# Row norms from products with ones and block products of 64 columns, in a two-layer diffusion backbone

## The reference

```python
def rmsnorm(x, g):
    y = x * rsqrt(mean(x * x, axis=-1) + 1e-6)
    return y * g
a = rmsnorm(x, norm_g) * (1 + scale) + shift
```

```python
q_dec, k_inv = q * exp(b), k * exp(-b)        # b: running sum of log gates in the chunk
att = where(tril, q_dec @ k_inv.T, 0)         # 64 x 64 in each chunk
o = att @ v + q_dec @ state_before_chunk
```

## Time and profile before

| | us |
|---|---|
| median of 3 runs | 1732.68 (1732.04 to 1733.84) |
| profiled execution, own time | 1733.48 |
| its span in the trace | 1731.8 |
| PE busy | 1633.6 (94%) |
| DVE busy | 621.9 (36%) |
| POOL busy | 601.2 (35%) |
| ACT busy | 516.8 (30%) |
| mean granted clock of PE | 0.968 |

### The profile page before, as it was taken

The page is one execution under the profiler, slowest core; times in us unless marked ns, Lnnn a source line. Parts: engine busy times, 40 slices in busy tenths (PEclk is TensorE's granted clock), DMA queues, the critical chain, the costliest instruction groups (busy, mean ns, idle before and its releaser), DMA issues. The chain is left out here.

```text
span 1731.8 us, 22476 instructions
## 1 busy us (share of the span) xinstructions
PE 1633.6 (94%) x9900; PEld 1371.8 (79%) x9900; DVE 621.9 (36%) x731; ACT 516.8 (30%) x560; POOL 601.2 (35%) x434
## 2 busy tenths in 40 slices
PE   6999999998799999999999997999977899999997
PEld 3888787877588888888888886788865688888885
DVE  5543334443441121211211125769985411111112
ACT  4343243322231110111111122477772321121122
POOL 2122211212213232332423244144464355455452
PEclk9899999999899999999999998999998899999999
DMA  9223334222224333233323222022212133333322
GB/s 338 82 86 110 88 84 122 74 74 80 67 73 123 98 98 98 89 107 101 105 87 98 92 89 88 25 73 73 72 50 73 49 98 97 98 97 98 97 79 79
DMA packets 199316, 160.63 MB, mean 93 GB/s; under 512 B 7234, under 2 KB 193972, under 8 KB 199220
## 3 DMA queue, kind: packets, MB, share of 16 engines
q1 hardware_dynamic: 198832, 159.08, 29.8%
q10 hardware_dynamic: 388, 0.12, 0.0%
HBM read 157.08 MB, written 2.10 MB: 92 GB/s over the span
## 5 line engine op out<-in xcount | busy, mean ns | idle before, releaser
L492 POOL TENSOR_TENSOR w_lo<-raw,w_hi 128x512 fp32r<-128x512 f32 (+1 forms) x404 | 580.8, 1469 | 1103.9 <-ACT w_hi L963 1103.9
L541 PE MATMUL duo<-a_hi,w_hi 128*128 128x512 f32 x1648 | 493.6, 360 | 36.9 <-DVE a_lo L1535 17.9
L544 PE MATMUL duo<-a_lo,w_hi 128*128 128x512 f32 x1648 | 486.8, 355 | 0.0
L547 PE MATMUL duo<-a_hi,w_lo 128*128 128x512 f32 x1648 | 486.1, 355 | 0.0
L963 ACT ACTIVATE w_hi<-raw 128x2048 fp32r<-128x2048 f32 (+1 forms) x101 | 192.5, 1906 | 577.1 <-PE duo L547 576.7
L541 PEld LDWEIGHTS duo<-a_hi,w_hi 128*128 128x128 f32 x1648 | 271.1, 191 | 96.9 <-issue 45.7
L544 PEld LDWEIGHTS duo<-a_lo,w_hi 128*128 128x128 f32 x1648 | 271.2, 191 | 45.6
L547 PEld LDWEIGHTS duo<-a_hi,w_lo 128*128 128x128 f32 x1648 | 270.5, 191 | 45.7
L1587 DVE TENSOR_TENSOR hid<-duo,gate 128x1024 f32<-128x1024 f32 (+1 forms) x33 | 33.5, 1044 | 525.5 <-PE duo L547 525.5
L541 PE MATMUL duo<-h_hi,w_hi 128*128 128x512 f32 (+1 forms) x528 | 159.4, 356 | 0.0
L547 PE MATMUL duo<-h_hi,w_lo 128*128 128x512 f32 (+1 forms) x528 | 158.3, 354 | 0.0
(11 more groups left out here) (230 smaller groups left out, 1494.4 us busy)
## 6 DMA issues: line engine op xcount, KB each, us to landing
raw<-in_ffn_w_dram SPq DMA_DIRECT2D x120, 512.0 KB, 4.8
mod_ring<-in_w_mod_dram SPq DMA_DIRECT2D x80, 512.0 KB, 5.3
raw<-in_gla_w_in_dram SPq DMA_DIRECT2D x24, 512.0 KB, 4.8
raw<-in_lru_w_in_dram SPq DMA_DIRECT2D x16, 512.0 KB, 4.3
raw<-in_ffn_w_dram SPq DMA_DIRECT2D x16, 384.0 KB, 3.7
mod_first<-in_w_mod_dram SPq DMA_DIRECT2D x4, 1024.0 KB, 14.2
mod_second<-in_w_mod_dram SPq DMA_DIRECT2D x4, 1024.0 KB, 13.7
raw<-in_gla_w_out_dram SPq DMA_DIRECT2D x8, 512.0 KB, 5.1
```

The costliest lines, as they stand in the source:

```text
L492: pool.tensor_tensor(w_lo[b][:, k:k + 2, 0:cols], raw[b][:, k:k + 2, 0:cols], w_hi[b][:, k:k + 2, 0:cols].bitcast(F32), ALU.subtract).then ...
L541: pe.matmul(tile_out(ps, t, part, n), wh, act_hi[:, k, s:s + n], start=opens, stop=False, skip_group_check=True)
L544: pe.matmul(tile_out(ps, t, part, n), wh, act_lo[:, k, s:s + n], start=False, stop=False, skip_group_check=True)
L547: mm = pe.matmul(tile_out(ps, t, part, n), wl, act_hi[:, k, s:s + n], start=False, stop=last, skip_group_check=True)
```

## The change

For the norms:

- The fourth pair of tiles is no longer added on DVE. Its tiles are squared one by one, the first already when its own residual addition is done (new semaphore tile_added). PE multiplies a full block of ones (128 by 128) with sqsum and with the two squares, accumulating in PSUM, which gives the sum on all partitions at once (norm_sums). The small products, the reciprocal, the diagonal and the spreading product are gone.
- ACT turns the sum into the inverse root in place in PSUM, as exp(-0.5 ln(sum/1024 + eps)), for each part of the columns in turn; the table loaded ahead is the one with both functions.
- In ACT's residual_loop the last squares now come before the rounding of the coming weight chunk (and before a row copy), where they came after.
- sqsum is not cleared; the first pair is added directly. In the first norm PE now does all sums before the second section's products.

For the attention:

- att is computed as 64 by 64 blocks, one per chunk and direction (24 a head), at two column positions; its tile has half the columns, and so have the memset, the masked copies and the addition on DVE.
- The product of att with v_tok becomes two blocks per pair of chunks, each of 64 rows and 64 columns, on the diagonal of the array.
- POOL copies the mask's other half instead of clearing two corners.

```diff
-            def token_sums(n, parts):
+            def norm_sums(n, parts):
                 q = ("stat", n)
-                pe.wait_ge(summed, SUMMED[n])
                 duo_wait(q)
-                for t in range((parts[-1][1] + parts[-1][2]) // P):
-                    mm = pe.matmul(duo(q)[:, 1, 2 * t:2 * t + 2], sqsum[:, t * P:(t + 1) * P], ones[:, 0:2], start=True,
-                                   stop=True, skip_group_check=True)
-                mm.then_inc(token_summed, 1)
-
-            def spread(n, parts):
-                q = ("stat", n)
-                pe.wait_ge(diag_ready, n + 1)
-                for part, s, w in parts:
-                    mm = pe.matmul(tile_out(duo(q), 0, part, w), ones[:],
-                                   rdiag[:, s // P:(s + w) // P].rearrange("p t n -> p (t n)"), start=True, stop=True)
+                for i, src in enumerate((sqsum, sq[1][:, 0], sq[1][:, 1])):
+                    if i:
+                        pe.wait_ge(squared, 5 * n + 3 + i)
+                    else:
+                        pe.wait_ge(summed, 3 * n + 3)
+                    for part, s, w in parts:
+                        mm = pe.matmul(tile_out(duo(q), 0, part, w), ones[:], src[:, s:s + w], start=i == 0, stop=i == 2,
+                                       skip_group_check=True)
                 done(mm)
...
-            token_sums(0, BOTH)
+            norm_sums(0, BOTH)
             pe.wait_ge(mod_ready, 1)
             second_products(0)
-            spread(0, BOTH)
...
                 for j in range(12):
                     d, tau = j // 6, j % 6
-                    mm = pe.matmul(flat(q)[:, j * P:(j + 1) * P], k_inv[:, d, tau * P:(tau + 1) * P],
-                                   q_dec[:, d, tau * P:(tau + 1) * P], start=True, stop=True, skip_group_check=True)
+                    for c in range(2):
+                        n = 2 * tau + c
+                        mm = pe.matmul(flat(q)[CHUNK * c:CHUNK * (c + 1), j * CHUNK:(j + 1) * CHUNK],
+                                       k_inv[:, d, n * CHUNK:(n + 1) * CHUNK], q_dec[:, d, n * CHUNK:(n + 1) * CHUNK],
+                                       start=True, stop=True, tile_position=(0, CHUNK * c), skip_group_check=True)
...
                 for tau in range(TT):
-                    pe.matmul(flat(q)[:, tau * 256:(tau + 1) * 256], att[:, tau], v_tok[:, tau], start=tau % 2 == 0,
-                              stop=False, skip_group_check=True)
+                    for c in range(2):
+                        r = CHUNK * c
+                        pe.matmul(flat(q)[r:r + CHUNK, tau * 256:(tau + 1) * 256], att[r:r + CHUNK, tau],
+                                  v_tok[r:r + CHUNK, tau], start=tau % 2 == 0, stop=False, tile_position=(r, r),
+                                  skip_group_check=True)
...
-            def square(pair, n, width):
-                if pair >= 2:
-                    act.wait_ge(summed, pair - 1)
-                act.activation(sq[pair % 2][:, :, 0:width], xres[:, 2 * n:2 * n + 2, 0:width], ACT.Square
-                               ).then_inc(squared, 1)
+            def square(norm, n, width):
+
+                if n >= 2:
+                    act.wait_ge(summed, 3 * norm + n - 1)
+                if n < 3:
+                    act.activation(sq[n % 2][:, :, 0:width], xres[:, 2 * n:2 * n + 2, 0:width], ACT.Square
+                                   ).then_inc(squared, 1)
+                    return
+                for t in range(2):
+                    if t == 0 and norm:
+                        act.wait_ge(tile_added, norm)
+                    elif norm:
+                        wait_moved(act, (("out", 0, 3), ("w2", 0, 2, 3), ("out", 1, 3))[norm - 1])
+                    act.activation(sq[1][:, t, 0:width], xres[:, 6 + t, 0:width], ACT.Square).then_inc(squared, 1)
 
             def prep(layer, which, parts):
 
                 n = 2 * layer + which
-                q = ("stat", n)
-                act.wait_ge(token_summed, n + 1)
-                tiles = (parts[-1][1] + parts[-1][2]) // P
-                act.activation(rms[:, 0, 0:tiles], duo(q)[:, 1, 0:2 * tiles:2],
-                               ACT.Sqrt, bias=eps[:, 0:1], scale=1.0 / D).then_inc(rooted, 1)
+                wait_done(act, ("stat", n))
+                for part, s, w in parts:
+                    ps = tile_psum(("stat", n), 0, part)
+                    steps.link(act.activation(ps, ps, ACT.Ln, bias=eps[:, 0:1], scale=1.0 / D))
+                    act.activation(ps, ps, ACT.Exp, scale=-0.5).then_inc(rooted, 1)
...
                 for n, name in enumerate(names):
                     ahead = {v: k for k, v in CH.items()}.get(CH[name] + 2)
+                    if norm is not None and n == 3:
+                        square(norm, n, width)
                     if ahead is not None:
                         high(ahead, name)
                     if of == ("out", 0) and n == 3:
                         row_copy(6, 0)
-                    wait_moved(act, name)
-                    if pair is not None:
-                        square(pair + n, n, width)
+                    if norm is None or n < 3:
+                        wait_moved(act, name)
+                    if norm is not None and n < 3:
+                        square(norm, n, width)
...
-            act.preload_act_table_set("sqrt_and_others")
+            act.preload_act_table_set("natural_log_exp_and_others")
             prep(0, 1, BOTH)
...
-                tiles = width // P
-                dve.wait_ge(rooted, n + 1)
-                steps.link(dve.reciprocal(rms[:, 1, 0:tiles], rms[:, 0, 0:tiles]))
-                if n == 0:
-                    dve.wait_ge(consts_made, 1)
-                dve.tensor_tensor(rdiag[:, 0:tiles], ident[:].unsqueeze(1).broadcast_to([P, tiles, P]),
-                                  rms[:, 1, 0:tiles].unsqueeze(2).broadcast_to([P, tiles, P]), ALU.mult
-                                  ).then_inc(diag_ready, 1)
                 wait_done(dve, ("stat", n))
+                dve.wait_ge(rooted, ROOTED[n] + len(parts))
...
-            def residual_loop(of, layer, place_, parts, pair=None, permuted=False):
-                if pair is not None:
-                    clear_sum()
+            def residual_loop(of, layer, place_, parts, norm=None, permuted=False):
```

70 lines of the change are left out of this document (35 added, 35 removed).

## The result

The changed kernel takes **1712.8 us** (median of four runs, 1710.97 to 1715.97) against 1732.36 of the kernel before beside it (1730.04 to 1733.84). The ratio is 0.989, its 95% interval 0.9871 to 0.9909: 19.6 us less, with the interval reaching from about 16 to 22. A second series of the same kernel on another chip gave 1712.14 and 0.9869. The profiled execution took 1713.71, against 1733.48 before: 19.8 less, and that is the difference that the traces have to explain.

The account below looks back on a forecast made before the run. PE was taken as the bound, busy 1633.6 of 1731.8 us. Terms -5.4 - 5.9 - 3.7 + 1.0 - 0.7 - 0.4 = -15.1, with 0.8 off the profiled 1733.48, gave 1717.6 us; range 1711 to 1727.

Parts of the forecast that it names:

- Second norm, 5.4: Second norm: first normed tile at 466.75 instead of 472.15, 5.4 us less, with ACT last and PE 2 us earlier.
- Third, 5.9: Third norm: first normed tile at 1074.55 instead of 1080.48, 5.9 us less, by the same chain without a row copy.
- Fourth, 4.1 less 0.4: Fourth norm: normed tile 4.1 us earlier, less 0.4 for a_lo running beside POOL's w_lo work, so 3.7 less.
- First norm, +1.0: First norm: sums ahead of the second section's products start the main products 1.0 us later, bounds 0 and +4.1.
- Clearing the sum, 0.7: Ahead of the first residual additions: the memset of 0.70 us goes, 0.7 less.
- Heads, 0.4: Attention heads: att 0.15 less, v_tok blocks 0.15 less, block form changes 0.2 more; four heads 0.4 us less.
- A: Heads: block loads go side by side, att 1.3 instead of 2.6 us per head, 5.2 less over four, 1712.4; chance 0.17.
- The clock, no gain counted: Behind the norms: main products again begin at the lower level, 1.2 of 2.4 GHz, so no gain there.
- Rival B: Norms: the clock falls while squares are awaited and PE ends last; norms gain less, first norm +3, 1722.5; chance 0.16.
- C: Heads: the blocks' weight loads aren't hidden; four heads cost +24.4 us instead of -0.4, 1742.4; chance 0.06.
- D: Norms: logarithm and exponential don't share a table; ten more loads of 1.28, 13 us, 1730; chance 0.02.

Follow-up runs that it names:

- e9: The changed kernel once more, with nothing changed, for a second time and trace: 1712.14 us, ratio 0.9869 of the kernel before.
- e3: The changed kernel with all 24 att blocks of a head at one column position (half of att wrong): 1719.83 us, one run.
- e2: The kernel before with only the two block products of the heads from the change, norms untouched: 1728.21 us, ratio 0.9978.
- e4: The changed kernel with ACT rounding the next weights before the last squares and copying the row behind the exponentials: 1709.21 us, ratio 0.9859.
- e5: The changed kernel with 14 unused products of 256 columns behind the sums of norms two to four: 1712.05 us, ratio 0.9884.
- e10: The kernel of e11 with unused products in three further gaps of PE (6, 4 and 30): 1701.9 us, ratio 0.9818 of before.
- e11: The changed kernel with rounding before squares, section products before first sums, nine unused products per later norm, earlier DVE start on latent columns; second series: 1706.0 us, 0.9841.

## Why the prediction was right

The forecast of 1717.6 had the side and, within the range of 1711 to 1727, the time; it was 4.8 us too slow, and the 1712.8 lie below the 1714 to 1722 that I gave the forecast as summed. By its own steps, in the one pair of traces:

- **Second norm, 5.4:** 5.8 measured. The second square ended 3.07 us after the start of the last additions (455.75), as forecast (460.6 - 457.53). Rounding, row copy and table load ended at 6.67, not 6.82. The four PSUM passes took 2.16 with the last hop, not 2.4: that is the mis-sized part, 0.24. PE wasn't last, by 1.7 us (forecast 2).
- **Third, 5.9:** 6.3. **Fourth, 4.1 less 0.4:** 4.3 at the normed tile, less 0.55 for the a_lo beside POOL's work (1.30 instead of 0.75), and 3.7 at PE: as forecast, by the mechanism forecast.
- **First norm, +1.0:** +1.6, inside the bounds of 0 and 4.1. The sums ended at 32.78 instead of 32.3 and the section's products at 34.64 instead of 34.0. In the trace of after it is gone at 97 us, at least 1.1 of it by the clock within the v products; in e9, the same kernel, it isn't. I had carried a delay at the start through to the end without asking what lies between, and that varies by 2.4 us between executions with the same start.
- **Clearing the sum, 0.7:** 0.9.
- **Heads, 0.4:** 3.4. This is the step that missed, and the one rival that came true (A). The price of 0.055 per record for att is right for blocks at one position (0.059 in e3), and wrong for alternating ones (0.030). The group gave 1.15 us a head in three heads and 0.26 in the first, where a wait for k_tok of 0.72 took its place. The v_tok blocks gave 0.05 each, not 0.15. I had both ends of the term (1.3 and 2.6; 1.55 came) and chose the wrong one. Even with it, 48 x 0.055 = 2.64 against 24 x 0.112 = 2.69 is 0.05 less and not 0.15. The row that I set aside as unable to tell, the narrow blocks of the earlier trace rows at 0.026, was the nearest after all; it too has more than one column position, though no run tested that for blocks of 32 columns. And the claim that no row shows two loads side by side was true of the rows and not of the trace, in which L792's loads start in pairs.
- **The clock, no gain counted:** the forecast was that the main products begin at the lower level, and they do. In the pair of traces 3.2 us instead of 6.1 of them ran low, worth 1.6; but the same gap left 5.4 in e3 and the old gap 4.3 in e2, so this is not shown to be a gain of the change.
- **Not foreseen:** 2.5 us lost in the first FFN. It took away most of what the missed part of the heads gave. So some of the nearness of 1717.6 and 1712.8 is luck: without it the kernel would have been at about 1710, below my range (1712.8 - 2.5, an estimate from the traces). The clock ahead of head 0 and behind the second norm was luck the other way, up to 3.3 us; without either the kernel would have been near 1713.6 (an estimate again).

Terms and measurement: -15.0 in three norms became -15.7; -0.1 ahead of them became -4.9; then -1.6 by the clock, +2.5 in the FFN, and -0.5 in three small pieces, in all -20.2 at the last main product.

Rival B (PE last) didn't happen in after, but it was near: e4 took 2.0 us of ACT's work out of the chain and PE was last by 0.9. The clock stayed high through the sums, also where B wanted it to fall. C and D didn't happen: no block was slower than the product that it replaced, and no table was loaded between the passes.

## What to carry to other kernels

Price small blocks by whether neighbours lie at different positions of the array, not by their width or load alone: 48 such records took 1.55 us alternating and 2.94 at one position. Behind each gap of the engine that bounds the kernel, read the granted clock too, but in more than one trace of the same kernel: low stretches came and went between executions and moved single stretches by 1 to 2.4 us, as much as the terms that one wants to read. Where unused products keep the clock high, look whether another engine can feed the faster pace; behind two of three norms DVE couldn't. When a serial chain crosses engines, count how long each of them waits for its first input: work that must be done anyway (here the rounding) belongs in that wait, ahead of the chain and not behind its first link.

## What was unexpected of the hardware

- Two 64-column blocks with the same 128 rows overlapped their loads and products, with starts 0.006 us apart: 0.030 us per record, against 0.059 at one position and 0.112 for a full block of 128 columns.
- Unused products kept the clock at its high level over waits of 6 to 14 us (14 of them in e5, 30 in e10; with nine it fell once, in e11), and they delayed nothing. What they brought was read by stretch: about 2.1 us behind three norms in e5 and 2.3 us ahead of the fourth norm in e10.
- Where the clock is low differs with nothing changed: in the v products of head 0 the lower level lasted 3.4 us in one trace of the changed kernel and 5.9 in the other. Behind one and the same gap of 12.6 us it lasted 2.8 to 5.4 us into the main products, in five traces of four kernels.
- A chunk of identical products at full clock has two durations, 16.63 and 16.94 us in most of the first FFN. The pattern came back in one repeated kernel (539.72 and 539.73) and nearly so in another (539.71 and 539.09). Its cause is open, and it moves the total by up to 2.5 us, as much as half a norm.
